# Start of a two-layer hybrid trunk on eight cores: order of the small loads, three wide query/key/value pieces, convolution weights behind x tile 3

## The reference, cut to what matters

```python
for layer in range(2):
    h = rmsnorm(x, norm1_g)
    u, q, k, v, gb, gc, gh = split(h @ w_in)            # 256 + 3*384 + 3*384 columns
    y_pool = pool_mix(u, windows 2/4/8/16) @ pool_w * pool_scale
    q, k = rope(rmsnorm(q, q_norm_g)), rope(rmsnorm(k, k_norm_g))   # per head of 64
    y_attn = merge(dilated_attention(g, q, k, v) for g in 3 groups of 2 heads)
    y_conv = gb * conv3(gc * gh, conv_w)                # causal, width 3
    x = x + concat(y_pool, y_attn, y_conv) @ w_out
    x = x + square(relu(rmsnorm(x, norm2_g) @ w_up)) @ w_down
```

## Time and profile before

| what | value |
|---|---|
| median of 3 runs | 1606.62 us (1606.47, 1606.62, 1822.35) |
| the profiled execution | 1609.26 us; span of its slowest core (core 5) 1607.4 us |
| spans of the 8 cores | 1584.9 to 1607.4 us |
| TensorE busy | 1469.7 us, 91% of the span |
| VectorE, ScalarE, GpSimd busy | 792.7, 581.7, 296.4 us |
| software queue (GpSimd's DMAs) | 59904 packets, 54.07 MB written |

### The profile page before, as it was taken

How to read it: one execution, slowest core, us unless ns; L and a number is a source line. 1 busy time by engine, 2 the same in 40 slices (tenths; PEclk the granted TensorE clock), 3 DMA queues, 4 the chain that set the end, 5 groups by cost and what they waited for, 6 DMA issues and landing times.

```text
span 1607.4 us, 26634 instructions; the slowest of 8 cores (1584.9 to 1607.4 us)
## 1 busy us (share of the span) xinstructions
PE 1469.7 (91%) x8614; PEld 721.9 (45%) x8614; DVE 792.7 (49%) x1210; ACT 581.7 (36%) x1267; POOL 296.4 (18%) x524
## 2 busy tenths in 40 slices
PE   2679996699999999999998999659999999999998
PEld 1335554354444444444454555424444444444443
DVE  1547664585443344344556676447544344334433
ACT  2676444484112111114455555347611211211210
POOL 3446543201000000001016765220000000000000
PEclk9779998699999999999999999869999999999999
DMA  8932216669536034009152321837741601500012
GB/s 138 205 72 29 26 29 137 136 176 156 97 74 110 13 52 75 4 4 154 57 127 43 39 25 36 171 70 203 126 111 53 118 26 28 98 4 4 40 79 96
DMA packets 91937, 130.16 MB, mean 81 GB/s; under 512 B 28920, under 2 KB 62194, under 8 KB 91418
## 3 DMA queue, kind: packets, MB, share of 16 engines
q0 software_dynamic: 59904, 54.07, 24.7%
q1 hardware_dynamic: 30986, 52.50, 9.9%
q10 hardware_dynamic: 912, 21.88, 5.3%
HBM read 159.64 MB, written 44.75 MB: 127 GB/s over the span
## 4 chain that ended last, share of the span: by engine, by line
PE 85%; DMA 4%; ACT 4%; issue 3%; DVE 2%; SPq 2%; POOL 1%; ACTq 0%; DVEq 0%; POOLq 0%
PE psum L682 82%; DMA kv_p<-big 2%; PE psum L834 2%; DMA big<-xs 1%; ACT big L815 1%; PE psum L1219 1%; SPq L794 0%; DMA conv_s<-big 0%; DVE big L1168 0%; ACT big L1271 0%; ACT big L1269 0%; PE psum L1392 0%; ACT big L838 0%; DVE big L823 0%; POOL big L1185 0%
## 5 line engine op out<-in xcount | busy, mean ns | idle before, releaser
L682 PE MATMUL psum<-big 128*128 128x512 bf16 (+10 forms) x7730 | 1419.9, 345 | 76.4 <-DVE big L1275 17.4
L682 PEld LDWEIGHTS psum<-big 128*128 128x128 bf16 (+5 forms) x7730 | 667.8, 101 | 791.3 <-issue 160.0
L1583 ACT ACTIVATE big<-psum 128x512 f32<-128x512 f32 (+1 forms) x320 | 165.3, 518 | 681.8 <-PE psum L682 673.7
L1585 DVE TENSOR_TENSOR big<-psum,big 128x512 bf16<-128x512 f32 (+1 forms) x320 | 187.9, 591 | 281.5 <-ACT big L1583 281.1
L1608 DVE TENSOR_TENSOR big<-psum,big 128x512 f32<-128x512 f32 (+1 forms) x272 | 187.9, 691 | 243.3 <-PE psum L682 243.1
L823 DVE SCALAR_TENSOR_TENSOR big<-big 128x1024 bf16<-128x1024 f32 (+1 forms) x68 | 87.8, 1292 | 71.2 <-ACT big L819 70.1
L742 POOL DMA_DIRECT2D big<-w_up x16 | 12.2, 764 | 514.7 <-PE psum L682 509.6
L815 ACT ACTIVATE big<-big 128x1024 bf16<-128x1024 f32 (+1 forms) x68 | 72.0, 1059 | 51.8 <-DVE big L1608 21.7
L834 PE MATMUL psum<-big 128*128 128x128 bf16 (+1 forms) x544 | 44.0, 228 | 45.8 <-DVE big L823 40.2
L838 ACT COPY big<-psum 128x1024 bf16<-128x1024 bf16 (+1 forms) x68 | 65.4, 969 | 22.8 <-PE psum L834 21.9
L834 PEld LDWEIGHTS psum<-big 128*128 128x128 bf16 (+1 forms) x544 | 36.1, 103 | 63.3 <-issue 54.5
(11 more groups left out here) (80 smaller groups left out, 634.0 us busy)
## 6 DMA issues: line engine op xcount, KB each, us to landing
big<-xp SPq DMA_DIRECT2D x32, 512.0 KB, 13.8
big<-w_up POOLq DMA_DIRECT2D x16, 1024.0 KB, 12.6
big<-w_down POOLq DMA_DIRECT2D x16, 1024.0 KB, 15.2
kv_s<-c ACTq DMA_DIRECT2D x8, 2040.0 KB, 13.3
xpark<-big SPq DMA_DIRECT2D x16, 512.0 KB, 3.0
big<-xpark SPq DMA_DIRECT2D x16, 512.0 KB, 16.3
yp<-big SPq DMA_DIRECT2D x16, 512.0 KB, 2.6
big<-c POOLq DMA_DIRECT2D x26, 256.0 KB, 4.3
```

Of the source, the lines that this page charges most:

```text
L682: S.op("pe", lambda e: e.matmul(out, lhsT=lhsT, rhs=rhs, start=start, stop=stop, skip_group_check=skip), reads=reads, writes=writes, cost=n)
L1583: S.op("act", lambda e: e.activation(out=RL[ri][:, 0:L], in_=bank(pi)[:, 0:L], func=AF.Relu), reads=[("ps", pi)], writes=[("rl", ri)], cos ...
L1585: S.op("dve", lambda e: e.tensor_tensor(out=at[:, fc, 0:L], in0=bank(pi)[:, 0:L], in1=RL[ri][:, 0:L], op=ALU.mult), reads=[("ps", pi), ("r ...
```

## The change

- The cost of a DMA issue on the SyncE and ScalarE queues in the planner's table goes from 0.06 to 0.5 us, and the table's sizes of the conv_w and norm-gain loads go up.
- x tiles 0 to 3 come ahead of the row GBC; the sample rows (tile 16) come behind x tile 7. The constants have a lower priority.
- `load_smalls` issues conv_w first, then q_norm_g and k_norm_g with one DMA each in place of two, then pool_scale.
- The q, k and v columns of w_in are loaded as three pieces of 384 columns, the order is wa 0, wa 2, wa 3, wa 1, q, k, v, and every `qkv_tile` waits for all three. The moving operand of its matmuls takes 128 columns from each.
- wa 2, wa 3 and wa 1 are issued with the buffer of x tile 3, `("xr", 3)`, as something that they read, so GpSimd's queue waits for the landing of that tile.
- `conv_item` waits for wa 1 only ahead of its last projection.
- In layer 1 the q piece is issued after wa 1, and k and v after the `up` matmuls of part 3.

```diff
@@ -167,7 +167,7 @@
         o.dma_val = self.dma_slots[slot]
         o.idx = len(self.ops[queue])
         t = self._deps(o, reads, writes)
-        self.ft[queue] = t + (0.9 if queue == "pool" else 0.06)
+        self.ft[queue] = t + (0.9 if queue == "pool" else 0.5)
         t0 = max(self.dma_ft[queue], t + 0.7)
         both = max(0.0, max(v for q, v in self.dma_ft.items() if q != queue) - t0)
         took = nbytes / DMA_RATE
@@ -533,10 +533,10 @@
-    GQK = ca.take([256], F32, *[("gqk", i) for i in range(4)])
+    GQK = ca.take([256], F32, ("gqk", 0), ("gqk", 1))
...
-    K_GQ = [("gqk", i) for i in range(4)]
+    K_GQ = [("gqk", i) for i in range(2)]
...
@@ -571,16 +571,15 @@
-    WQ = [ARENA[:, 12288 + 3072 * g:15360 + 3072 * g].rearrange("p (a b) -> p a b", a=8) for g in range(3)]
+    WQ = ARENA[:, 12288:21504].rearrange("p (j a b) -> p j a b", j=3, a=8)
...
-    for g in range(3):
-        for j in range(3):
-            areg(("wq", g, j), 12288 + 3072 * g + 128 * j, 384, 8, 128)
+    for j in range(3):
+        areg(("wq", j), 12288 + 3072 * j, 3072, 1, 3072)
...
@@ -736,10 +735,12 @@
             S.dma(lambda e: e.dma_start(out=o_pool_s[:, :, 0:7, :], in_=spool[:, :, 8:15, :]), slot="c2cp", queue="act")
 
     def wload(dst, src, key, nbytes, done, *after):
+        rd = [a for a in after if not isinstance(a, Ev)]
         for a in after:
-            yield a
+            if isinstance(a, Ev):
+                yield a
         yield "pool"
-        S.dma(lambda e: e.dma_start(out=dst, in_=src), writes=[key], slot=key, queue="pool", nbytes=nbytes)
+        S.dma(lambda e: e.dma_start(out=dst, in_=src), reads=rd, writes=[key], slot=key, queue="pool", nbytes=nbytes)
         fire(done)
 
     def load_wa(l, j, *after):
@@ -750,12 +751,9 @@
             c0, a0 = 1408 + 384 * (j - 1), 256 + 384 * (j - 1)
             R_.add(wload(WA[:, :, a0:a0 + 384], wv[:, :, c0:c0 + 384], ("wa", j), 3 << 19, ev(l, "wa", j), *after))
 
-    def load_wq(l, g, *after):
+    def load_wq(l, j, *after):
         wv = w_in[l].rearrange("(c p) n -> p c n", p=128)
-        ev_need(3, l, "wq", g)
-        for j in range(3):
-            c0 = 256 + 384 * j + 128 * g
-            R_.add(wload(WQ[g][:, :, 128 * j:128 * j + 128], wv[:, :, c0:c0 + 128], ("wq", g, j), 1 << 19, ev(l, "wq", g), *after))
+        R_.add(wload(WQ[:, j], wv[:, :, 256 + 384 * j:640 + 384 * j], ("wq", j), 3 << 19, ev(l, "wq", j), *after))
 
     def load_wo(l, *after):
         wv = w_out[l].rearrange("(c p) n -> p c n", p=128)
@@ -786,17 +784,16 @@
             S.dma(lambda e, g=g, pc=pc, hf=hf: e.dma_start(out=PWBD[hf * 64:(hf + 1) * 64, pc, hf * 64:(hf + 1) * 64], in_=pool_w[l, g]),
                   writes=[("pwbd", g)], slot=("pwbd", g), queue="pool", nbytes=16384)
         yield "sp"
+        for k in range(3):
+            for c in range(3):
+                S.dma(lambda e, k=k, c=c: e.dma_start(out=CONVW[:, c, k:k + 1], in_=conv_w[l, k, c * 128:(c + 1) * 128].rearrange("(p o) -> p o", o=1)), writes=[("convw", 3 * c + k)], slot=("sm_cw", 3 * c + k), nbytes=16384)
+        for j in range(2):
+            src = k_norm_g if j else q_norm_g
+            S.dma(lambda e, j=j, src=src: e.dma_start(out=GQK[:, 128 * j:128 * j + 128].rearrange("p (h c) -> p h c", h=2),
+                                                      in_=src[l].partition_broadcast(128).unsqueeze(1).to_broadcast([128, 2, 64])),
+                  writes=[("gqk", j)], slot=("sm_gq", j), nbytes=65536)
         for pc in range(2):
-            S.dma(lambda e, pc=pc: e.dma_start(out=PSCALE[:, pc:pc + 1], in_=pool_scale[l, pc * 128:(pc + 1) * 128].rearrange("(p o) -> p o", o=1)),
-                  writes=[("pscale", pc)], slot=("sm_ps", pc), nbytes=512)
-        for cc in range(3):
-            for k in range(3):
-                S.dma(lambda e, cc=cc, k=k: e.dma_start(out=CONVW[:, cc, k:k + 1], in_=conv_w[l, k, cc * 128:(cc + 1) * 128].rearrange("(p o) -> p o", o=1)),
-                      writes=[("convw", 3 * cc + k)], slot=("sm_cw", 3 * cc + k), nbytes=512)
-        for j in range(4):
-            src = q_norm_g if j < 2 else k_norm_g
-            S.dma(lambda e, j=j, src=src: e.dma_start(out=GQK[:, 64 * j:64 * j + 64], in_=src[l].partition_broadcast(128)),
-                  writes=[("gqk", j)], slot=("sm_gq", j), nbytes=32768)
+            S.dma(lambda e, pc=pc: e.dma_start(out=PSCALE[:, pc:pc + 1], in_=pool_scale[l, pc * 128:(pc + 1) * 128].rearrange("(p o) -> p o", o=1)), writes=[("pscale", pc)], slot=("sm_ps", pc), nbytes=512)
         fire(ev(l, "smalls"))
 
     def norm_task(t, xt, xkey, gev, done, pre=None, after=(), used=None):
@@ -984,7 +981,7 @@
         yield ev(l, "smalls")
         for e_ in ht_wait(l, "ht1", b):
             yield e_
-        for j in (1, 2, 3):
+        for j in (2, 3):
             yield ev(l, "wa", j)
         if smp:
             yield ev(l, "zs", cc)
@@ -1039,6 +1036,7 @@
             yield "dve"
             S.op("dve", lambda e: e.scalar_tensor_tensor(out=v3(CACC[ci]), in0=sz(k, k + Lq), scalar=CONVW[:, cc, k:k + 1], in1=v3(CACC[ci]),
                                                          op0=ALU.mult, op1=ALU.add), reads=[zkey, kc] + K_CW, writes=[kc], cost=0.32 + n / 960)
+        yield ev(l, "wa", 1)
         pgb = yield want("D", 1, DL[0])
         yield "pe"
         proj(256 + 128 * cc, l, b, pgb)
@@ -1102,7 +1100,8 @@
         W = WINS[g]
         yield ev(l, "open")
         yield ev(l, "smalls")
-        yield ev(l, "wq", g)
+        for j_ in range(3):
+            yield ev(l, "wq", j_)
         if g == 2 and not smp:
             yield ev(l, "slot0")
         sel = []
@@ -1125,11 +1124,11 @@
         pqk = pall[:, :, 0:256]
         pvv = pall[:, :, 256:384]
         pbk = [("ps", pb + j_) for j_ in range(J)]
-        wk = [("wq", g, j_) for j_ in range(3)]
+        wk = [("wq", j_) for j_ in range(3)]
         for j, (cs, ts) in enumerate(sel):
             htk = [("ht", t) for t in ts]
             for d in range(8):
-                mm(bank(pb + j)[0:R, 0:384], HT[:, d, cs], WQ[g][:, d, :], d == 0, d == 7, wk + htk, [("ps", pb + j)], pe(384))
+                mm(bank(pb + j)[0:R, 0:384], HT[:, d, cs], WQ[:, :, d, 128 * g:128 * g + 128], d == 0, d == 7, wk + htk, [("ps", pb + j)], pe(384))
         yield ev(l, "scratch")
         yield ev(l, "rope")
         si = yield tk(P_SQ)
@@ -1641,20 +1640,19 @@
             ev_need(2, l, "x3", t)
 
     R_.add(load_gbc(norm1_g[0], ev(0, "g1")), -60)
-    order0 = [0, 1, 2, 3, 16] + list(range(4, 16))
-    for t in order0[:5]:
-        R_.add(norm_task(t, None, None, ev(0, "g1"), ev(0, "ht1", t), pre=(xp[128 * t:128 * t + 128, :] if t < 16 else xs), used=ev(0, "xrdone")), -50 + 0.1 * t)
+    order0 = list(range(8)) + [16] + list(range(8, 16))
+    for t in order0[:4]:
+        R_.add(norm_task(t, None, None, ev(0, "g1"), ev(0, "ht1", t), pre=xp[128 * t:128 * t + 128, :], used=ev(0, "xrdone")), -70 + 0.1 * t)
     load_wa(0, 0)
-    R_.add(load_consts(), -49)
+    R_.add(load_consts(), -30)
     R_.add(load_smalls(0), -48)
-    load_wq(0, 0)
-    load_wa(0, 2)
-    load_wa(0, 3)
-    load_wa(0, 1)
-    load_wq(0, 1)
-    load_wq(0, 2)
-    for t in order0[5:]:
-        R_.add(norm_task(t, None, None, ev(0, "g1"), ev(0, "ht1", t), pre=xp[128 * t:128 * t + 128, :], used=ev(0, "xrdone")), -40 + 0.1 * t)
+    load_wa(0, 2, ("xr", 3))
+    load_wa(0, 3, ("xr", 3))
+    load_wa(0, 1, ("xr", 3))
+    for j in range(3):
+        load_wq(0, j)
+    for i, t in enumerate(order0[4:]):
+        R_.add(norm_task(t, None, None, ev(0, "g1"), ev(0, "ht1", t), pre=(xp[128 * t:128 * t + 128, :] if t < 16 else xs), used=ev(0, "xrdone")), -55 + 0.1 * i)
     for l in range(DEPTH):
         phase_a(l)
         load_wo(l, ev(l, "a2a"))
@@ -1688,12 +1686,12 @@
             if b == 0 and fb == 3 and l + 1 < DEPTH:
                 d2, u2 = ev(l, "downmm", 2), ev(l, "upmm", 2)
                 load_wa(l + 1, 0, d2, u2)
-                load_wq(l + 1, 0, d2, u2)
                 load_wa(l + 1, 2, d2, u2)
                 load_wa(l + 1, 3, d2, u2)
                 load_wa(l + 1, 1, d2, u2)
-                for g in (1, 2):
-                    load_wq(l + 1, g, d2, ev(l, "upmm", 3))
+                load_wq(l + 1, 0, d2, u2)
+                for j in (1, 2):
+                    load_wq(l + 1, j, d2, ev(l, "upmm", 3))
             if fb < 3 and b < 4:
                 R_.add(cache_shift(l, *shifts[4 * fb + b], ev(l, "at", k)))
             if k == 6 and l + 1 < DEPTH:
```

## The result

The changed kernel takes 1615.95 us (median of 4 runs, 1615.48 to 1617.65), against 1606.6: the ratio is 1.006, with an interval of 1.0036 to 1.0085, so 6 to 14 us slower. I had forecast 10 us less. The profiled execution's span is 1613.8 us, on core 6. On the median core the last norm of layer 0 is 6 us later, and the end 8 us later.

A forecast was written before the change was run, and what follows sets the result against it. It took TensorE's idle time at layer 0's start, from loads delayed by norm-gain broadcasts, as the bound. -4 - 8 - 3 + 5 = -10 us on 1609.3 gave 1599.3, median 1597 us; 8-in-10 range 1582 to 1618.

The forecast's parts named there:

- Step 4: TensorE in layer 0's start: earlier convolution work gains 4 us from 24 to 83, 8 to 130, 3 by clock.
- Step 5: End of layer 0's mixer phase, 240 to 320 us: convolution done early is no filler later; 5 us lost again.
- What bounds the kernel: Early TensorE idle time, 24 to 130 us: late loads behind four norm-gain broadcasts of 256 B to 128 partitions.
- Step 1: SyncE's order: tile 4 replaces the sample rows, lands about 45; ScalarE's wait keeps its length, slow stretch unchanged.
- Rival (a): Layer 0's start: the slow stretch vanishes, everything to 83 us moves up some 14 us; 1583 us, chance 0.15.
- Step 2: The weights' queue: wider runs 1.2 to 1.43 times faster; wa 3 at about 49, wa 1 56, v 75 to 78.
- Step 3: SyncE's queue: tile 7 waits for wa 1 until about 56; tile 15 issued 93 to 98, attention 3 to 8 later.
- my sum: Terms in us: -4 from 24 to 83, -8 from 83 to 130, -3 for clock, +5 at the phase's end.
- rival (b): Mixer tail takes all the gain, since attention sets the phase's end and starts no earlier; 1604 to 1612, chance 0.22.
- Small terms: 384-column matmuls 0 to 2 ns each, layer 1 -3 to +4 us, reshuffled order plus or minus 8; all taken as 0.
- (c): Slower: x tiles late if wa 1 lands past 60; 4 us by 83, 8 in the tail; 1619 us, chance 0.14.

The follow-up runs named there:

- h1: The changed kernel in its own order, waits kept, with the two norm-gain broadcasts replaced by one-row loads spread by matmuls; 1604.98 us in one run.
- f4: The kernel before with its four norm-gain broadcasts made one-row loads spread by two matmuls, in a newly planned order; 1605.4 us, ratio 0.9978.
- g1: The kernel before in its own order, with norm gains and conv_w loaded as whole rows and spread by TensorE; 1597.0 us, ratio 0.9941.
- h2: The same kernel as g1 once more, timed in more rounds against the kernel before; 1597.2 us, ratio 0.9941.
- g2: The changed kernel in its own order, without GpSimd's wait for x tile 3 and SyncE's wait for w_in; 1615.7 us, ratio 1.0067.
- e4: The changed kernel with wa 2, 3, 1 not tied to x tile 3's buffer and q, k, v issued ahead of them; 1627.05 us, ratio 1.0128.
- f2: The kernel before with only the wide w_in pieces, their new order and their waits, in both layers; 1628.7 us, ratio 1.012.
- f1: The kernel before with only the planner's cost of a SyncE issue raised from 0.06 to 0.5 us; 1616.1 us, ratio 1.0052.

## Why the prediction was wrong

Steps 4 and 5 failed: TensorE did not take the work when its weights had landed, and what it lost from 130 to 320 us was more than twice the 5 us booked.

**What bounds the kernel.** Right: the small loads' slow stretch, and I had taken the four broadcasts for its cause. h1 and f4, where nothing else is loaded differently, show it, and g1 agrees. But the copies are not why the change is slower. Without them it still is: h1 took 1604.98 us where g1 and h2 took 1597.0 and 1597.2, with the last norm 5.5 and 5.7 us later and the mixer's end 6.6 and 8.5, about as with them (6.3 and 7.5).

**Step 1** was right in the order, the wait of ScalarE (18.15 us) and in the stretch staying whole. With half the DMAs but the same 512 copies it is as slow as before. Rival (a) fell with it.

**Step 2** was right: wa 3 at 48.1 (said 49), wa 1 at 57.1 (56), v at 76.2 (75 to 78), all on core 6; over the eight cores wa 3 landed at 42.0 to 51.1. The Trainium skill's page "DMA: Bandwidth & Descriptors", section "Specifications", gives 512 B as the smallest transfer at line rate; that shorter runs go at half rate was my own assumption. With it v would have landed at about 70 on core 6. On cores 0, 2, 5 and 7 v did land at 70.1 to 72.1, but wa 1 was earlier there too (50.9 to 53.0). The time between the two decides: 17.9 to 19.6 us over the eight cores, where the same bytes took 21.7 to 24.5 before. That is the ratio of the earlier trace rows at its low end and not a half. Packets under 512 B in the whole run fell from 28920 to 10232 and the software queue's from 59904 to 47424, and the kernel is no faster for it.

**Step 3** was right in the wait, its length and what follows: tile 7 out at 57.2, tile 15 at 98.4 (said 93 to 98). It was wrong in the effect: g2 takes the wait away, and the last norm and the time stay. And its end failed: attention starts 19.8 us later and not 3 to 8, and "TensorE has other work then" did not hold, since TensorE is busy 5.4 us less from 130 to 240 than before.

**Step 4 failed.** I let TensorE take gc and gh when wa 3 had landed (49), but its list is fixed and has tile 4's transposes and a pooling product first, so gc began at 55.3 and gh at 59.3. From 24 to 83 that gives 31.8 and not 37.4 us; from 44 to 60 alone it is 6.1 where I had 15. The sum was wrong by itself, too: it puts those 15 us of work between 49 and 60, which is 11 us, and with 11 it comes to 33.4 (5.4, 11 and 17), no gain over 33.3. Then 83 to 130 had 37.4 and not 43: query/key/value tiles wait for v at 76.2 and for the lists, and the first one's sum of squares runs at 96.9 us, where it ran at 55.3 (medians of the cores). The 12 us gained by my sum became 0.4 (69.2 us busy against 68.8). The clock rose to 0.89 from 83 to 130, as I had hoped, and fell to 0.53 from 44 to 60, where the earlier trace rows have 0.71; what that is worth, -3 in my sum, no run separates.

**Step 5 failed in its size and its reason.** I booked 5 us as lost again, because 130 to 240 was full and attention would start only a little later. TensorE's busy time fell by 5.4 us from 130 to 240 and by 5.7 from 240 to 320, 11 in all. In the terms of the sum, -4 became +1.5, -8 became -2 and +5 became +11: 10.6 us behind by 320, where the mixer's end is 7.5 later. Over the cores of a single run before, the mixer's end follows the last norm about one for one: core 2 has 95.0 and 304.5, core 3 108.6 and 321.0. By the table it lies 214.1 to 217.8 us behind it in eleven of fourteen kernels. The last norm opens attention, and attention ends the phase, as rival (b) said: its last exponential is 7.9 to 9.1 us ahead of the mixer's end in all fourteen kernels, while convolution's last product came 13.5 us earlier in the changed kernel than before. The last norm is 6.3 us later, which is most of the 7.5. What ties the two at a fixed distance is not shown: attention's first exponential is 19.8 us later, and in e4 and f2 the distance grew.

**Small terms.** The matmul of 384 columns, before and with its three runs:

```profile
L682 PE MATMUL psum<-big 128*128 128x384 bf16 x768 | 148.9, 353 | 3.8 <-DVE big L1168 1.7 <-ACT big L1269 1.1 <-ACT big L1271 0.8
```

```profile
L681 PE MATMUL psum<-big 128*128 128x384 bf16 x768 | 152.0, 358 | 10.6 <-DMA big<-w_in 4.1 <-ACT big L1268 2.8 <-ACT big L1270 1.1
```

358 ns, where it was 353, is over my bound of 2 ns each and makes 3.1 us; but the total of all matmuls at that line is 1418.1 us against 1419.9, so taking 0 was fair. The 4.1 us of idle for w_in are the waits for late pieces. Layer 1's mixer is 1.4 us longer, inside my bounds; but the table has it up to 8.4 us longer than before and never shorter, in kernels with new orders and, by 3.2 and 6.1 us, in the old one. What sets it stays open.

**The rivals.** The outcome is nearest to (c), which I gave 0.14, by its sign and at 9.3 of its 12 us. Of its mechanism only the late x tiles came true (tile 15 issued at 98.4, not 105). wa 1 landed at 57 and not past 60, its point of decision; from 60 to 83 TensorE was busy 19.3 us, as before; and x was not held up beside the long runs (0.93 MB from 66 to 72, where it was 0.84). So the nearness is in part luck. The later last norm was in my own step 3 as "3 to 8 us"; booked one for one and without step 4's gain it makes 1610 to 1615.

## What to carry to other kernels

Where the order of instructions is fixed when the program is built, data that lands earlier helps only an engine whose list has the consumer next; read the list before costing a transfer. Find the event that opens the long chain (here the last norm), and price a change by how that event moves as well as by the busy time it adds nearby; here that held in eleven of fourteen kernels. To test a change of data or waits, hold the order still: f1, which rewrote the order and nothing else, took 0.5% (8 us) more.

## What the runs showed of the hardware

- Four DMAs that send one row of 256 B to 128 partitions, on all eight cores at about the same time, held the cores' traffic to 66 to 155 GB/s for 20 us; with each row sent once and spread by TensorE the same stretch moved 200 to 209 (f4 and g1). The DMA engines of core 5 were busy in 0.62 of the stretch, so it is not their time that ran out. Eight cores reading the same few bytes is my guess at the cause; that was only argued, and no run changes the number of cores.
- The harm fell on one core of each neighbouring pair: 58 to 98 GB/s beside 113 to 204, in nine kernels of nine. Without the copies no core was under 180. Why it is one of two is open.
- Two DMAs with a repeated source did as much harm as four with as many copies.
- Without the copies the cores stay closer in step: the last norm spreads over 1.9 us (g1), 3.6 (h2) and 5.3 (f4) in place of 13.6, and over 6.0 (h1) in place of the changed kernel's 9.1.
